# Expert weights on one Trainium2 core: a ring of nine 2 MB slots taken in turn, with loops over three experts

## What is computed

```python
def _moe(xt, w_router, b_router, w_up_gate, b_up_gate, w_down, b_down):
    t, d = xt.shape
    logits = (xt @ w_router + b_router).astype(jnp.float32)
    top_vals, top_idx = lax.top_k(logits, TOP_K)
    gates = jax.nn.softmax(top_vals, axis=-1)
...
    def expert_block(args):
        xb, e = args
        hgu = xb @ w_up_gate[e] + b_up_gate[e]
        x_glu = jnp.minimum(hgu[:, :D_EXPERT], SWIGLU_LIMIT)
        x_lin = jnp.clip(hgu[:, D_EXPERT:], -SWIGLU_LIMIT, SWIGLU_LIMIT)
        hact = x_glu * jax.nn.sigmoid(SWIGLU_ALPHA * x_glu) * (x_lin + 1.0)
        return hact @ w_down[e] + b_down[e]

    ys = lax.map(expert_block, (xs, block_e)).reshape(n_slots, d)
    return jnp.zeros((t, d), xt.dtype).at[slot_tok].add(ys * slot_gate[:, None].astype(xt.dtype))
```

## Time and profile before

| what | us |
|---|---|
| median of 3 runs | 2009.18 (2007.88 to 2009.27) |
| profiled execution | 2011.88 |
| its span, first to last instruction | 2010.2 |
| PE busy | 1793.4 (89%) |
| DVE, ACT, POOL busy | 767.8, 494.9, 187.6 |
| last barrier ahead of the expert stage to its end | about 187 to 1140 |

### The profile page before, as it was taken

The page is one execution under the profiler, slowest core; times in us unless marked ns, Lnnn a source line. Parts: engine busy times, 40 slices in busy tenths (PEclk is TensorE's granted clock), DMA queues, the critical chain, the costliest instruction groups (busy, mean ns, idle before and its releaser), DMA issues. The chain is left out here.

```text
span 2010.2 us, 28826 instructions
## 1 busy us (share of the span) xinstructions
PE 1793.4 (89%) x11522; PEld 1114.6 (55%) x11522; DVE 767.8 (38%) x1348; ACT 494.9 (25%) x787; POOL 187.6 (9%) x141
## 2 busy tenths in 40 slices
PE   7887999989988888888898889988998999888997
PEld 5664333333333333333333368977997778847996
DVE  7924311111110111111011274945554674435555
ACT  4522200000000000000000236444452324124442
POOL 3511000000000000000000044330000105000000
PEclk9998999999999999999999999998998999888998
DMA  7334799999999999999999645437532432126530
GB/s 264 131 147 184 306 428 428 428 428 428 428 427 428 428 428 428 428 428 428 427 428 428 284 186 208 183 100 277 194 140 57 158 105 86 44 75 262 206 127 32
DMA packets 104401, 554.14 MB, mean 276 GB/s; under 512 B 17377, under 2 KB 27618, under 8 KB 78898
## 3 DMA queue, kind: packets, MB, share of 16 engines
q1 hardware_dynamic: 104338, 553.26, 68.1%
HBM read 551.15 MB, written 2.10 MB: 275 GB/s over the span
## 5 line engine op out<-in xcount | busy, mean ns | idle before, releaser
L1151 PE MATMUL banks<-front,xsT 128*64 128x512 f32 x2048 | 458.7, 597 | 42.5 <-DMA front<-in_w_up 42.0
L1151 PEld LDWEIGHTS banks<-front,xsT 128*64 128x64 f32 x2048 | 143.0, 137 | 350.7 <-issue 264.3
L1326 DVE TENSOR_SCALAR glu<-banks 128x512 f32<-128x512 f32 x32 | 22.1, 692 | 657.7 <-PE banks L1158 657.7
L1189 PE MATMUL banks<-front,hT 128*64 128x512 f32 x1024 | 230.2, 603 | 22.0 <-ACT hT L1242 22.0
L1189 PEld LDWEIGHTS banks<-front,hT 128*64 128x64 f32 x1024 | 71.5, 138 | 158.6 <-issue 130.5
L2000 PE MATMUL banks<-f_xT_hi,f_w_hi 128*128 128x256 f32 x512 | 146.7, 287 | 4.2 <-DVE f_w_lo L2085 4.2
L2000 PE MATMUL banks<-f_xT_hi,f_w_lo 128*128 128x256 f32 x512 | 146.6, 286 | 0.0
L2000 PE MATMUL banks<-f_xT_lo,f_w_hi 128*128 128x256 f32 x512 | 146.5, 286 | 0.0
L1238 ACT ACTIVATE sig<-glu 128x512 f32<-128x512 f32 x32 | 20.1, 630 | 495.7 <-DVE glu L1326 495.7
L2000 PEld LDWEIGHTS banks<-f_xT_hi,f_w_hi 128*128 128x128 f32 x512 | 100.1, 196 | 7.1 <-DVE f_w_lo L2085 5.2
L1456 POOL TENSOR_TENSOR p_w_lo<-p_w_raw,p_w_hi 128x1024 fp32r<-128x1024 f32 x4 | 12.4, 3105 | 961.7 <-ACT p_w_hi L1500 961.6
(11 more groups left out here) (421 smaller groups left out, 2754.2 us busy)
## 6 DMA issues: line engine op xcount, KB each, us to landing
front<-in_w_up SPq DMA_DIRECT2D x128, 2048.0 KB, 24.8
front<-in_w_down SPq DMA_DIRECT2D x64, 2048.0 KB, 20.4
ring<-in_ffn_w SPq DMA_DIRECT2D x30, 2048.0 KB, 8.8
m_raw<-in_w_in SPq DMA_DIRECT2D x7, 2048.0 KB, 8.8
ring<-in_sgu_in SPq DMA_DIRECT2D x7, 2048.0 KB, 7.7
ring<-in_sgu_out SPq DMA_DIRECT2D x4, 2048.0 KB, 7.6
w_arena<-in_w_rkv SPq DMA_DIRECT2D x4, 2048.0 KB, 13.7
m_raw<-in_w_out SPq DMA_DIRECT2D x2, 2048.0 KB, 7.9
```

The lines of the kernel that those rows point to most:

```text
L1151: ins = nc.tensor.matmul(c.banks[CAP * h:CAP * (h + 1), bank, :], xsT[:, k, :], up_slot[k // 2][:, o:o + BANK], start=k == 0, stop=False)
L1189: ins = nc.tensor.matmul(c.banks[CAP * h:CAP * (h + 1), DOWN, :], hT[:, at:at + CAP], down_slot[half][:, o:o + BANK], start=k == 0, stop=k ...
L1326: v.tensor_scalar(glu[:, :], c.banks[:, GLU, :], LIMIT, None, ALU.min).then_inc(glu_ready, 1)
```

## The change

- The ring has nine slots (`RING` = 9): the six in `front` and three in a new buffer, `more_slots`. Load number n goes to slot n mod 9, so an item's six loads start at a different slot each time, and the pattern repeats after three items.
- To make room, `rest` becomes a view of the ninth slot, and `glu`, `sig`, `lin`, `act_h` become views of `xT`, which the router is done with by then. Their shapes are as before.
- Each slot has its own landing semaphore, `landed[at]`.
- SP issues items 1 to 3 in straight code, then nine passes of a loop over three items, then a loop over the remaining items (item 31 alone here). The wait ahead of a load is for the use nine loads back. The first two loads of item 1 wait for nothing, and the third waits for `third_part`, since its slot holds `rest`. In the last loop (`late_item`) the wait is still for the use six loads back.
- PE runs item 0, ten passes of a loop over three items, reads the item count, and runs a loop over the remaining items. ACT and DVE keep their loops over one item.

```diff
+RING = FRONT + 3
...
-        up_slot = [c.slot(i) for i in UP_SLOT]
-        down_slot = [c.slot(i) for i in DOWN_SLOT]
-
-        rest = sb("rest", [P, TC, D])
+        more = sb("more_slots", [P, (RING - FRONT) * SLOT])
+        slots = [c.slot(i) for i in UP_SLOT + DOWN_SLOT] + [more[:, i * SLOT:(i + 1) * SLOT] for i in range(RING - FRONT)]
+        landed = c.up_in + c.down_in + [sem(f"slot_in{i}") for i in range(FRONT, RING)]
+        rest = slots[RING - 1][:, 0:TC * D].rearrange("p (c n) -> p c n", c=TC)
...
-        glu = sb("glu", [P, BANK])
-        sig = sb("sig", [P, BANK])
-        lin = sb("lin", [P, BANK])
-        act_h = sb("act_h", [P, BANK])
+        glu, sig, lin, act_h = (c.xT[:, 2 * i:2 * i + 2, :].rearrange("p k t -> p (k t)") for i in range(4))
...
-                def item(i, e):
-                    for q in range(UPS):
-                        sp.wait_ge(up_used, i * UPS + (q + 1 - UPS))
-                        c.load_up(sp, e, q)
-                    for h in range(DOWNS):
-                        sp.wait_ge(down_used, i * DOWNS + (h + 1 - DOWNS))
-                        c.load_down(sp, e, h)
...
+                def item(n, one):
+                    for s in range(FRONT):
+                        if not isinstance(n, int) or one > 1 or s > 2:
+                            ago, last = divmod(s - RING, FRONT)
+                            if last < UPS:
+                                sp.wait_ge(up_used, n * (3 * UPS) + ((one + ago) * UPS + last + 1))
+                            else:
+                                sp.wait_ge(down_used, n * (3 * DOWNS) + ((one + ago) * DOWNS + last + 1 - UPS))
+                        elif s == 2:
+                            sp.wait_ge(third_part, TC)
+                        load(n * 3 + one, s, (FRONT * one + s) % RING)
+
+                def late_item(i, e):
+                    for s in range(FRONT):
+                        if s < UPS:
+                            sp.wait_ge(up_used, i * UPS + (s + 1 - UPS))
+                        else:
+                            sp.wait_ge(down_used, i * DOWNS + (s - UPS + 1 - DOWNS))
+                        load(e, s, (FRONT + s) % RING)
...
-                item(1, 1)
+                for one in (1, 2, 3):
+                    item(0, one)
+                with sp.Fori(1, (E - 2) // 3) as n:
+                    for one in (1, 2, 3):
+                        item(n, one)
                 items = count(sp)
-                with sp.Fori(2, items) as i:
-                    item(i, listed_at(sp, i + EXPERT_AT, E - 1))
+                with sp.Fori(E - 1, items) as i:
+                    late_item(i, listed_at(sp, i + EXPERT_AT, E - 1))
...
                 item(0, True)
+                with pe.Fori(0, (E - 2) // 3) as n:
+                    for one in (1, 2, 3):
+                        item((n, one), False)
                 items = count(pe)
-                with pe.Fori(1, items) as i:
+                with pe.Fori(E - 1, items) as i:
                     item(i, False)
```

More of the change, by code:

```diff
@@ L141, in slot, with load_up, load_down @@
         return self.front[:, i * SLOT:(i + 1) * SLOT]
[L143 to L149, removed]
+    def load_up(self, sp, e, q, slot=None, landed=None):
+        sp.dma_start(slot or self.slot(UP_SLOT[q]), self.dram["w_up"][bass.ds(e * P, P), q * SLOT:(q + 1) * SLOT]).then_inc(
+            landed or self.up_in[q], 16)
+    def load_down(self, sp, e, h, slot=None, landed=None):
+        sp.dma_start(slot or self.slot(DOWN_SLOT[h]), self.dram["w_down"][bass.ds(e * (2 * P) + h * P, P), :]).then_inc(
+            landed or self.down_in[h], 16)
     def load_expert_tables(self, sp):
@@ L1052, in count, with times @@
             return eng.value_load(work_list[0:1, 0:1], min_val=E, max_val=E + MAX_EXTRA)
+        def times(i, m, a):
+            if isinstance(i, tuple):
+                n, one = i
+                return n * (3 * m) + (one * m + a)
+            return i * m + a
         with nc.Block() as block:
@@ L1056, in _, with load @@
             def _(sp):
-                def item(i, e):
-                    for q in range(UPS):
-                        sp.wait_ge(up_used, i * UPS + (q + 1 - UPS))
-                        c.load_up(sp, e, q)
-                    for h in range(DOWNS):
-                        sp.wait_ge(down_used, i * DOWNS + (h + 1 - DOWNS))
-                        c.load_down(sp, e, h)
+                def load(e, n, at):
+                    if n < UPS:
+                        c.load_up(sp, e, n, slots[at], landed[at])
+                    else:
+                        c.load_down(sp, e, n - UPS, slots[at], landed[at])
+                def item(n, one):
[13 more added lines that the diff above has]
+                            sp.wait_ge(up_used, i * UPS + (s + 1 - UPS))
+                        else:
+                            sp.wait_ge(down_used, i * DOWNS + (s - UPS + 1 - DOWNS))
+                        load(e, s, (FRONT + s) % RING)
                 sp.dma_start(chooser[:, :], c.dram["chooser"]).then_inc(chooser_in, 16)
@@ L1136, in open_sums, with weights @@
                     pe.wait_ge(c.b_down_in, 32)
+                def weights(i, n):
+                    one = i[1] if isinstance(i, tuple) else 0 if isinstance(i, int) else 1
+                    lap, at = divmod(FRONT * one + n, RING)
+                    if isinstance(i, tuple):
+                        pe.wait_ge(landed[at], i[0] * 32 + 16 * (lap + 1))
+                    elif isinstance(i, int):
+                        pe.wait_ge(landed[at], 16)
+                    else:
+                        pe.wait_ge(landed[at], i * 16 + 16 * (lap + 1 + 2 * ((E - 2) // 3) - (E - 1)))
+                    return slots[at]
                 def item(i, first):
-                    pe.wait_ge(xs_ready, i + 1)
-                    pe.wait_ge(halves_read, i + 1)
+                    pe.wait_ge(xs_ready, times(i, 1, 1))
+                    pe.wait_ge(halves_read, times(i, 1, 1))
                     quarters = [(bank, h, bank * D + h * BANK) for bank in (GLU, LIN) for h in range(2)]
@@ L1151, in item @@
                             ins = nc.tensor.matmul(c.banks[CAP * h:CAP * (h + 1), bank, :], xsT[:, k, :],
-                                                   up_slot[k // 2][:, o:o + BANK], start=k == 0, stop=False)
+                                                   up[:, o:o + BANK], start=k == 0, stop=False)
                         if k % 2 and k < KC - 1:
                             ins.then_inc(up_used, 1)
-                    pe.wait_ge(chosen_ready, i + 1)
+                    pe.wait_ge(chosen_ready, times(i, 1, 1))
                     pe.wait_ge(bias_split, 3)
@@ L1163, in item @@
                         open_sums()
-                    pe.wait_ge(y_ready, i + 1)
-                    pe.wait_ge(spreadT_ready, i + 1)
+                    pe.wait_ge(y_ready, times(i, 1, 1))
+                    pe.wait_ge(spreadT_ready, times(i, 1, 1))
                     combine(False)
-                    pe.wait_ge(spread_ready, i + 1)
+                    pe.wait_ge(spread_ready, times(i, 1, 1))
                     for tc in range(TC):
@@ L1171, in item @@
                     ins.then_inc(spread_turned, 1)
[L1172 to L1175, removed]
+                    pe.wait_ge(hT_ready, times(i, 1, 1))
+                    gather(times(i, 1, 1))
+                    pe.wait_ge(h_ready, times(i, 1, 1))
+                    pe.wait_ge(xs_ready, times(i, 1, 2))
                     for j in range(KC // 2):
@@ L1179, in item @@
                     ins.then_inc(h_turned, 1)
-                    pe.wait_ge(hT_ready, i + 2)
-                    pe.wait_ge(spreadT_ready, i + 2)
+                    pe.wait_ge(hT_ready, times(i, 1, 2))
+                    pe.wait_ge(spreadT_ready, times(i, 1, 2))
                     for k in range(KC):
@@ L1185, in item @@
                         if j == 0:
-                            pe.wait_ge(c.down_in[half], i * 16 + 16)
+                            down = weights(i, UPS + half)
                         for h in range(2):
@@ L1189, in item @@
                             ins = nc.tensor.matmul(c.banks[CAP * h:CAP * (h + 1), DOWN, :], hT[:, at:at + CAP],
-                                                   down_slot[half][:, o:o + BANK], start=k == 0, stop=k == KC - 1)
+                                                   down[:, o:o + BANK], start=k == 0, stop=k == KC - 1)
                         if j == KC // 2 - 1:
```

2 lines of the change are left out of this document (1 added, 1 removed).

## The result

The changed kernel took 1989.37 us in the median of 4 runs (1984.44 to 1989.87), against 2009.22 us for the kernel before (4 runs, 2007.88 to 2011.23). The ratio is 0.9901, 95% interval 0.9885 to 0.9916, a gain of 19.9 us (16.9 to 23.1). The direction was right; the forecast of 1994.5 us and its range from 1991.0 missed by 5 us and by 1.6 us. A gain of 14.7 us lies outside the interval.

A forecast was written before the change was run, and what follows sets the result against it. The prediction took the expert stage's transfers at 428 GB/s as the bound. Three loads ahead gave -14.7 us, all other terms 0, so 2009.18 becomes 1994.5 us; own range 1992 to 1997, for 8 in 10 1991 to 2000.

The forecast's parts named there:

- Three loads ahead: Start of the expert stage: three 2 MB loads move before PE's first use of a slot, gaining 3 x 4.90 = 14.7 us.
- The gap at 230 us: Transfer gap of 2.1 us in 230 to 235 us, where load 10 waits for the first down half; said to stay.
- The rival that the gain is eaten ahead of item 0: Early loads stretch the router's chain before item 0 by as much as they bring; time near 2009.2 us, 6%.
- Rate of the transfers: Expert stage: loads keep 428 GB/s, 4.90 us per 2 MB load, six per item in 29.4 us; no change priced.
- a falling rate as a sign against it: Expert stage: the forecast is wrong if the DMA rate falls below 428 GB/s with nine slots.
- the case of more than three loads' gain: Rival: the gap at 230 us closes too, some 2 us, or later stages run better; 1991 to 1992 us, 4%.
- The stage's end: Sign in the profile after: the expert stage ends at about 1125 us, against 1139.6 before.
- PE keeps up: Expert stage: of PE's 42.0 us of transfer waits 14.7 go and 27.3 stay, so the gain is not cut.
- Time from issue to landing: Sign for up loads in the expert stage: about 24.8 + 14.7 = 39.5 us from issue to landing.
- The branch back: PE's loop of three items, taken as 0 us; rival that it stalls PE on code transfers, 2039 or 2215 us, 5%.
- The last item's old wait and the moved reads of the count: Loads 186 to 191 wait six uses back, and SP and PE read the item count later; cost 0 for both.
- The third load's margin: Load 8 is through at 209.4 us, 2.7 us to spare; rival that only two loads get ahead, 1999.4 us, 9%.

The follow-up runs named there:

- The old depth: Changed kernel with each load waiting for the use six loads back, none ahead of item 0; 2003.32 us against 2007.25 for the kernel before, ratio 0.998.
- two loads ahead: Changed kernel with each load waiting for the use eight loads back instead of nine; 1992.74 us, ratio 0.9926 to the kernel before.
- the run with own slots: Old-depth kernel, loops over three items kept, but each quarter and half sent to its own old slot in `front`; ratio 1.0006 to the kernel before.
- the second profile of the changed kernel: Changed kernel run again unaltered beside the follow-up kernels; 1987.17 us, ratio 0.9895 to the kernel before.

## Why the prediction was right and wrong

**Three loads ahead, 14.7 us: right.** The old depth and the changed kernel differ only in depth and early loads; from release to end they took 925.2 and 910.2 us, 15.0 apart, and with two loads ahead 915.0, 10.2 below the first. The expected steps are 14.7 and 9.8. The gap at 230 us stayed, as said. The rival that the gain is eaten ahead of item 0 did not come: the release stands 23.6 us behind the stage's start in both profiles.

**Rate of the transfers: the step that failed.** The sum rested on "at every later moment the transfers are three loads further" at the 4.90 us of before, and priced the new buffer at nothing, without naming it as a term. In its place stands: 63 of the 186 loads go to new places (43 up quarters and 20 down halves), 63 x 0.062 = 3.9 us. With it the sum is -18.6 us, which is what the trace shows from release to end (928.8 - 910.2), and 2009.2 becomes 1990.6, inside the measured interval. The text named a falling rate as a sign against it and had no case for a rising one; the case of more than three loads' gain, at 4% and 1991 to 1992, gave other reasons. The stage's end was forecast at about 1125 and came at 1117.0 us: 4.0 us of that are the stage's earlier start, the rest is this term.

**What is left, some 1 us** between 18.6 and the medians' 19.9, is less than the interval of either comparison (16.9 to 23.1 here). I leave it unexplained.

**The width of the range.** I took the scatter from three runs that happened to lie within 1.4 us. Later runs of the same kernel spread over more than 10 us. With the case of an unpriced buffer in it, the lower end would have had to be near 1988.

**PE keeps up: right.** 27.3 us of waits for up quarters were expected to be left, 29.6 were measured. The first wait came after 500 us, as expected. Most of the 2.3 us is in how the prediction used the row. By PE's timeline, 25 items stood 29.42 us apart before and 18 some 29.30 after; but for one item in between, those ahead of them stood 27.2 us apart. An item at the transfers' pace loses 2.2 us, but the row has only 1.76 of them (0.50 + 1.26): seven such items fewer take 12.3 us out of the row and not 14.7, which leaves 29.7. That it fits to 0.1 us is luck, since two items of the trace before lack a part of their waits.

**Time from issue to landing:** 39.5 us was expected for up loads. The stage's median is 34.9, since ahead of 500 us, while PE led, up loads took 21.4 us. In mid-stage (700 to 1060 us) they took 37.1 into `front` and 36.3 into `more_slots`, and down loads 39.7 and 39.6, near the 39.5 expected. The view of 240 to 1080 us:

```profile
front<-in_w_up SPq DMA_DIRECT2D x77, 2048.0 KB, 34.9
more_slots<-in_w_up SPq DMA_DIRECT2D x39, 2048.0 KB, 34.8
front<-in_w_down SPq DMA_DIRECT2D x38, 2048.0 KB, 39.2
```

**The branch back, 0 us: right.** Beside the run with own slots, the DMA view of 300 to 1080 us in the changed kernel has a single transfer of code, over some 26 items, and PE's waits in that stretch name no cause but DVE, ACT and the weights:

```profile
q1 hardware_dynamic: 22993, 334.98, 100.7%
q8 instruction: 1, 0.02, 0.0%
...
PE banks L1214 <- DVE xsT L1346: 24.5, 28, 0.9
PE banks L1188 <- DMA front<-in_w_up: 19.3, 24, 1.3
PE banks L1226 <- ACT hT L1282: 19.2, 28, 0.7
PE banks L1188 <- DMA more_slots<-in_w_up: 8.7, 11, 1.2
```

The Trainium skill (Runtime: NRT & Kernel Launch, Instruction fetch mechanics) says both that a branch out of a window of two pages stalls and that PE's instruction memory holds 2048 instructions. The trace agrees with the second: a body of 330 matmuls and as many weight loads went round without a stall. The feed-forward loop of the kernel before, had been the right row to ask. One figure of the prediction is wrong without harm: the code is longer by 330 matmuls and not by 220, since PE's program has the item five times where it had it twice. Between 183 and 1118 us the two traces have 8 and 4 packets of code.

**The last item's old wait and the moved reads of the count: right.** The last fourth quarter stood 29.24 us behind the one before it (1067.96 to 1097.20), no more than in mid-stage.

**The third load's margin: right in this trace, thinner than it looked.** Its 2.7 us of spare time came from PE's half clock ahead of the release. In the second profile of the changed kernel the clock was back earlier, the release came 20.9 us after the stage's start, and the transfers ran almost without a stop from load 8 into load 9 (380 GB/s at 205 to 210 us, 413 behind it). Nothing was lost yet: without the 1.7 us of its last down product, release to end is 910.0 us, against 910.2. A release still earlier would have found load 8 under way.

```profile
205.00:210.00 5.00, 4.66 (x22) 1.63 (x24) 4.04 (x9) 2.65 (x2) 0.00 (x0) 1.00 0.94 380
210.00:215.00 5.00, 5.00 (x34) 1.61 (x30) 2.51 (x4) 2.03 (x2) 0.00 (x0) 1.00 1.00 413
```

No version in these runs beats the changed kernel. Since the savings of the new places add up whatever the order, reordering the ring should bring nothing; the one such run, with the new places in reverse, had 1988.27 us and 910.1 from release to end.

## What to carry to other kernels

In a stage where the transfers run without a gap, a deeper ring gave here what it moved into an idle stretch ahead of the stage (15.0 us measured for three loads of 4.90): count the idle microseconds, count the loads that fit, multiply. Its depth alone did nothing to the rate, though it also closed a gap inside the stage where loads were not spent ahead of it (3.3 us). Waits of an engine inside the stage say only that the gain won't be cut. And a new buffer is a term of its own, even when everything written to it looks the same: with a saturated stream of 186 loads, 0.02 us a load is 4 us, so compare the rate to the third digit and leave room for it in the range.

## What was not expected of the hardware

- A 2 MB load into one on-chip buffer took 4.90 us and into another about 4.84 us, 1.3% less, with source, queue, depth and semaphores the same. The 4.84 is an estimate, 4.903 less 0.062, since no kernel had new places only (29.42, 29.36, 29.30 and 29.23 us an item with 0, 1, 2 and 3 such loads of 6).
- Eight loads of 2 MB queued on one engine's queue (39.7 us from issue to landing) moved data at the same rate as five: 29.30 us an item in the changed kernel, 29.29 with the old depth.
- The stage ahead of the experts, untouched by the change, ended at 183.26 us in one profile and at 188.12 in another of the same kernel.
